# Nine gate tiles of the second mixer: from mixed matmuls of 512 and 256 columns to 256 columns alone

## The chip, the cores and the metric

The kernel runs on one core of one Trainium2 chip. The metric is the device time of one execution in microseconds. Before the change the median of three runs is 976.09 us (975.73 to 976.19).

## The reference, cut to what matters

The reference runs three transformer layers over 256 tokens of width 1024, all in float32: a layer with a short convolution and a gated MLP, a layer with windowed attention and a gated MLP, and a last layer with a hybrid mixer and an MLP. The change lies in the hybrid mixer:

```python
proj = jnp.einsum("bsd,dc->bsc", u, w_in)
q, k, v, x_lru, g_lru, gate_attn, gate_lru = jnp.split(proj, list(SPLITS), axis=-1)
...
attn = moba_attention(qh, kh, to_heads(v))
y_attn = attn @ w_branch_attn
xc = causal_depthwise_conv(x_lru, conv_w, conv_b)
hl = rg_lru(xc, w_rg_a, b_rg_a, w_rg_i, b_rg_i, lru_lambda)
y_lru = (hl * jax.nn.gelu(g_lru)) @ w_branch_lru
merged = jax.nn.sigmoid(gate_attn) * y_attn + jax.nn.sigmoid(gate_lru) * y_lru
return merged @ w_out
```

The three gates, `g_lru`, `gate_attn` and `gate_lru`, are each 1024 columns of the product with `w_in`. There are 8 heads of attention; with 256 tokens and blocks of 256 each head is plain causal attention.

## The kernel before, in words

**Products.** Activations lie with features on the 128 partitions and tokens along the columns. For float32 accuracy every operand is split into a high part, rounded to the matmul's input format, and a low part, the rest. A product is the sum of three: high weights with high activations, high weights with low activations, low weights with high activations. A tile is 128 output features for 256 tokens, summed over 8 blocks of 128 input features. High and low activations of a block lie next to each other, 256 columns each.

**Two kinds of tile.** A narrow tile has three matmuls of 256 columns for each of the 8 blocks, 24 in all, into one half of a PSUM bank (`blocks`, lines 549, 551 and 553). A mixed tile (`whole_tile`) does the two products with high weights at once for the first six blocks, as one matmul of 512 columns into the whole bank (line 524); the low weights (line 522) and the last two blocks (lines 533 and 534) go in 256 columns into the first half. So it has 6 matmuls of 512 columns and 12 of 256. The two halves of its bank still have to be added: ScalarE copies the second half into `spill` (`spill_tile`, line 1136), and VectorE adds the first half to it (`sum_tile`, line 1675). A narrow tile's result VectorE copies out of the bank by itself (line 2092).

**Weights.** Each tile has one piece of weights of 128 x 1024. ScalarE rounds it into `whi` (line 1104) and VectorE subtracts to get `wlo` (line 1638). There are four places for pieces; that of tile n + 4 is made when tile n is done. The first operation behind a tile on ScalarE is the spill, if the tile is mixed, and then the rounding of that piece.

**The order in the second mixer.** A loop over `r` (on TensorE from line 944 on; tiles 0 to 59) goes through the tiles of its input projection in a fixed order: `x2`, `q2`, `k2`, `rg`, `v2`, and then the gates `g2` (36 to 43), `ga` (44 to 51) and `gl` (52 to 59). `beside(r)` puts the steps of attention behind certain tiles: scores (lines 904 and 905) of a new head behind every third one from 33 to 54, values (lines 931 to 933) and transposes (line 916) of earlier heads there too, with the first transposes behind tile 37 and the last values behind tile 59. Such a set of small matmuls is called a group here. The loop is followed by two projections of 8 tiles each, `ba` (the first `MIXED_BRANCH` = 2 tiles are mixed) and `bl`, and by the output projection `out2`.

`MIXED_GATES` names the gate tiles that are mixed. Before the change it holds ten: 36, 37, 38, 40, 43, 46, 49, 52, 55 and 58. All of them but 36 stand right behind a group; groups stand behind tiles 36, 37, 39, 42, 45, 48, 51, 54, 57 and 59. The engines ask `is_mixed(r)`, and offsets into the count of spills (`S0`) follow from the list's length.

**Other places that the prediction names.** In the attention layer's mixer (called the first mixer here), blocks of its output projection (`wo_blocks`, narrow) stand behind transposes (line 798); the second half of that projection is narrow tiles alone. In the first part of the last MLP (`mup_first`, lines 1031, 1032 and 1038) narrow matmuls follow a group that spreads a row of gains (line 1012); mixed tiles follow them.

Of the kernel before, what the change touches and what calls it, by code (L numbers as in the profile page):

```python
# [53 lines left out]
for _name, _n in BODIES:  # L54
# [10 lines left out]
AT = {name: 4 * B0[name] - R0 for name in ("x2", "q2", "k2", "rg", "v2", "g2", "ga", "gl", "ba")}  # L65
HEAD_AT = AT["v2"] + 5

MIXED_GATES = [r for r in range(AT["g2"], AT["ba"])
               if r == AT["g2"] or (r - HEAD_AT) % 3 == 1 or r == HEAD_AT + 5]
MIXED_BRANCH = 2  # L70

S0 = {}
# [1 line left out]
for _name, _n in (("bx", 4 * WIDE_BODIES), ("up0", 4 * WIDE_BODIES), ("qkv", 12), ("up1", 4 * WIDE_BODIES),  # L74
                  ("x2", 8), ("q2", 8), ("k2", 8), ("gates", len(MIXED_GATES)), ("ba", MIXED_BRANCH),
                  ("out2", 7), ("mup", 4 * WIDE_BODIES)):
# [46 lines left out]
def build(nc, bias_in_dram, x_in, stream, vecs_in, sinks_in, cons_in, out):  # L123
    with ExitStack() as ctx:
# [263 lines left out]
        def segment_of(r):  # L388
            return [name for name in AT if AT[name] <= r][-1]
# [23 lines left out]
        def is_mixed(r):  # L413

            return segment_of(r) in S0 or r in MIXED_GATES

# [1213 lines left out]
        def _(dve):  # L1630
# [41 lines left out]
            def sum_tile(at, slot, dst):  # L1672

                dve.wait_ge(spilled, at + 1)
                dve.tensor_tensor(dst, acc(slot), spill[:, slot, :], ALU.add).then_inc(emptied, 1)  # L1675
# [376 lines left out]
            for r in range(AT["ba"]):  # L2052
# [18 lines left out]
                else:  # L2071
# [16 lines left out]
                    elif is_mixed(r):  # L2088
                        sum_tile(S0["gates"] + MIXED_GATES.index(r), r % 4, dst)
                    else:  # L2090
# [429 lines left out]
```

## Time and profile before

| | |
|---|---|
| median of 3 runs | 976.09 us (975.73 to 976.19) |
| the profiled execution | 975.92 us |
| its span on the core | 973.9 us |
| TensorE busy | 967.8 us (99%) |
| VectorE busy | 692.0 us (71%) |
| ScalarE busy | 583.1 us (60%) |
| GpSimd busy | 267.0 us (27%) |

The profile names the engines PE (TensorE's matmuls), PEld (its weight loads), DVE (VectorE), ACT (ScalarE) and POOL (GpSimd). L524 is line 524. Matmuls overlap: one of 256 columns is given as some 276 ns long, while the next begins some 113 ns after it. So the pace is read from the distance between starts, and the sum of the durations is more than the time that passed.

### The profile page before, as it was taken

Reading aid. Unit: us, or ns where it says so; the run is one execution under the profiler, and the core shown is the slowest. Engines: PE = TensorE matmul, PEld = TensorE weight load, DVE = VectorE, ACT = ScalarE, POOL = GpSimd, SP = SyncE. Lnnn points to the kernel's source line nnn. Section 1 sums busy time; section 2 is a strip of 40 time slices with the busy share of each in tenths; the row PEclk is TensorE's granted clock in tenths of the full one; section 3 lists DMA queues with packets and bytes.
Section 4 is the critical chain, followed back from the end, with each engine's and each line's share of the span. In section 5 each row is a group of like instructions: output and inputs, shape, how many; then the busy total and the mean of one; then the engine's idle time right before and its main releaser. Section 6 shows DMA issues by size and latency. Waiting matters only on the chain.

```text
span 973.9 us, 20479 instructions
## 1 busy us (share of the span) xinstructions
PE 967.8 (99%) x7368; PEld 913.1 (94%) x7368; DVE 692.0 (71%) x1037; ACT 583.1 (60%) x1026; POOL 267.0 (27%) x241
## 2 busy tenths in 40 slices
PE   9999999999999999999999999999999999999998
PEld 7999999999998899999999999889999999998887
DVE  6987866665668788666655799997866877664443
ACT  7556754454557767555554587968484677664332
POOL 2431233220102222322201146642031545441000
PEclk9999999999999999999999999999999999999999
DMA  9785555545543235555556555554445536556531
GB/s 332 261 316 188 189 208 180 207 171 196 205 169 136 88 130 217 179 209 184 182 193 210 179 177 172 200 196 168 168 144 181 202 130 221 209 176 206 182 130 44
DMA packets 37714, 180.96 MB, mean 186 GB/s; under 512 B 3472, under 2 KB 7824, under 8 KB 19984
## 3 DMA queue, kind: packets, MB, share of 16 engines
q1 hardware_dynamic: 37504, 179.99, 52.6%
q8 instruction: 43, 0.70, 0.3%
q14 instruction: 23, 0.19, 0.1%
q10 hardware_dynamic: 144, 0.08, 0.0%
HBM read 179.01 MB, written 1.05 MB: 185 GB/s over the span
## 4 chain that ended last, share of the span: by engine, by line
PE 91%; DVE 5%; ACT 2%; issue 1%; POOL 0%; ACTq 0%; POOLq 0%
PE bank L553 21%; PE bank L549 19%; PE bank L551 19%; PE bank L547 5%; PE bank L524 4%; PE bank L590 4%; PE bank L591 4%; PE bank L589 4%; PE bank L522 3%; DVE wlo L1638 3%; PE bank L673 1%; DVE z L1675 1%; PE bank L534 1%; PE bank L533 1%; DVE bank L2020 1%
## 5 line engine op out<-in xcount | busy, mean ns | idle before, releaser
L1638 DVE TENSOR_TENSOR wlo<-raw,whi 128x1024 fp32r<-128x1024 f32 (+1 forms) x289 | 354.5, 1227 | 153.9 <-ACT whi L1104 153.3
L1104 ACT ACTIVATE whi<-raw 128x1024 fp32r<-128x1024 f32 (+2 forms) x289 | 302.2, 1046 | 217.3 <-PE bank L553 210.6
L549 PE MATMUL bank<-xa,whi 128*128 128x256 f32 x952 | 239.4, 276 | 0.0
L551 PE MATMUL bank<-xa,whi 128*128 128x256 f32 x952 | 239.3, 276 | 0.0
L553 PE MATMUL bank<-xa,wlo 128*128 128x256 f32 x1184 | 236.4, 277 | 0.0
L553 PEld LDWEIGHTS bank<-xa,wlo 128*128 128x128 f32 x1184 | 187.0, 188 | 7.6
L549 PEld LDWEIGHTS bank<-xa,whi 128*128 128x128 f32 x952 | 178.7, 188 | 0.0
L551 PEld LDWEIGHTS bank<-xa,whi 128*128 128x128 f32 x952 | 178.7, 188 | 0.0
L2250 POOL TENSOR_TENSOR gate<-act,rbc 128x256 f32<-128x256 f32 x44 | 68.9, 1567 | 158.2 <-ACT act L1270 153.0
L551 PE MATMUL bank<-ghid,whi 128*128 128x256 f32 x352 | 88.5, 276 | 0.0
L549 PE MATMUL bank<-ghid,whi 128*128 128x256 f32 x352 | 88.5, 276 | 0.0
L549 PE MATMUL bank<-xb,whi 128*128 128x256 f32 x336 | 87.2, 281 | 0.2 <-ACT rr L1482 0.2
L551 PE MATMUL bank<-xb,whi 128*128 128x256 f32 x336 | 85.9, 277 | 0.0
L1647 DVE TENSOR_TENSOR wlo<-raw,whi 128x1024 fp32r<-128x1024 f32 x40 | 49.2, 1231 | 45.9 <-ACT whi L1114 45.8
L547 PE MATMUL bank<-xa,whi 128*128 128x512 f32 x232 | 77.1, 403 | 0.0
L1114 ACT ACTIVATE whi<-raw 128x1024 fp32r<-128x1024 f32 x40 | 42.5, 1066 | 49.3 <-PE bank L591 33.1
L553 PE MATMUL bank<-xb,wlo 128*128 128x256 f32 x336 | 69.1, 277 | 0.0
L553 PE MATMUL bank<-ghid,wlo 128*128 128x256 f32 x352 | 68.6, 276 | 0.0
L524 PE MATMUL bank<-xa,whi 128*128 128x512 f32 x240 | 68.4, 393 | 0.1
L549 PEld LDWEIGHTS bank<-ghid,whi 128*128 128x128 f32 x352 | 66.1, 188 | 0.0
L551 PEld LDWEIGHTS bank<-ghid,whi 128*128 128x128 f32 x352 | 66.1, 188 | 0.0
L2231 POOL TENSOR_TENSOR ssum<-ssum,sq 128x256 f32<-128x256 f32 x39 | 35.8, 917 | 106.9 <-ACT sq L1146 106.5
(258 smaller groups left out, 1817.8 us busy)
## 6 DMA issues: line engine op xcount, KB each, us to landing
raw<-in_stream SPq DMA_DIRECT2D x137, 1024.0 KB, 4.8
raw<-in_stream SPq DMA_DIRECT2D x42, 512.0 KB, 4.9
raw<-in_stream SPq DMA_DIRECT2D x8, 768.0 KB, 4.1
bias<-in_bias SPq DMA_DIRECT2D x1, 3072.0 KB, 11.5
raw<-in_stream SPq DMA_DIRECT2D x8, 256.0 KB, 5.0
x<-in_x SPq DMA_DIRECT2D x4, 256.0 KB, 4.9
out<-x SPq DMA_DIRECT2D x3, 256.0 KB, 2.2
cons<-in_cons SPq DMA_DIRECT2D x1, 576.0 KB, 9.5
```

What stands on the lines that cost most here:

```text
L524: pe.matmul(dst, whi[:, slot, k, :], X[:, k, :, :], start=k == 0, stop=False)
L547: pe.matmul(dst, whi[:, slot, at + i, :], X[:, k, :, :], start=first and i == 0, stop=False)
L549: pe.matmul(narrow, whi[:, slot, at + i, :], X[:, k, 0, :], start=first and i == 0, stop=False)
L551: pe.matmul(narrow, whi[:, slot, at + i, :], X[:, k, 1, :], start=False, stop=False)
L553: ins = pe.matmul(narrow, wlo[:, slot, at + i, :], X[:, k, 0, :], start=False, stop=last and i == len(tiles) - 1)
L589: pe.matmul(dst[:, :], X[:, k0 + k, 0, cols], hi, start=first and k == 0, stop=False)
L590: pe.matmul(dst[:, :], X[:, k0 + k, 0, cols], lo, start=False, stop=False)
L1104: act.activation(whi[:, p, 0:kts, :].rearrange("p k m -> p (k m)"), src, ACT.Copy)\
L1114: act.activation(dst[:, p, :, :].rearrange("p (k m) c -> p k m c", k=2), k_pairs(raw[:, (b % 2) * 2 + p // 2, :], p % 2), ACT.Copy).then_i ...
L1638: dve.tensor_tensor(wlo[:, p, 0:kts, :].rearrange("p k m -> p (k m)"), src, whi[:, p, 0:kts, :].rearrange("p k m -> p (k m)").bitcast(F32) ...
L1647: dve.tensor_tensor(lo[:, p, :, :].rearrange("p (k m) c -> p k m c", k=2), k_pairs(raw[:, (b % 2) * 2 + p // 2, :], p % 2), hi[:, p, :, :] ...
L2250: pool.tensor_tensor(gate[:, m, :], act1[:, m, :], rbc[:], ALU.mult).then_inc(gate_ready, 1)
```

## The change

The list of mixed gate tiles is cut to its first, tile 36. The nine others are computed as narrow tiles, on TensorE, ScalarE (no spill) and VectorE (a copy in place of the sum). Nothing else changes.

```diff
-MIXED_GATES = [r for r in range(AT["g2"], AT["ba"])
-               if r == AT["g2"] or (r - HEAD_AT) % 3 == 1 or r == HEAD_AT + 5]
+MIXED_GATES = [AT["g2"]]
 MIXED_BRANCH = 2
```

## Rows read from the trace of the kernel before

**Rows 1.** The page's head: span, and busy time of each engine.

```profile
span 973.9 us, 20479 instructions
PE 967.8 (99%) x7368; PEld 913.1 (94%) x7368; DVE 692.0 (71%) x1037; ACT 583.1 (60%) x1026; POOL 267.0 (27%) x241
```

**Rows 2.** The page's chain of waits: shares of the span by engine.

```profile
PE 91%; DVE 5%; ACT 2%; issue 1%; POOL 0%; ACTq 0%; POOLq 0%
```

**Rows 3.** Busy time by windows, tiles 37 to 59, all engines.

```profile
core 0: us, PE busy (x) PEld busy (x) DVE busy (x) ACT busy (x) POOL busy (x), PEclk, DMA share, GB/s
643.98:719.12 75.14, 75.14 (x596) 72.34 (x595) 59.67 (x112) 50.34 (x94) 14.37 (x16) 1.00 0.47 158
```

**Rows 4.** Timeline of TensorE, tiles 40 to 42: start, length, line, operation, count.

```profile
654.12 0.49 PE L916 MATMUL bank<-cons,pr 128*128 128x128 f32 x3
654.37 0.95 PE L524 MATMUL bank<-xb,whi 128*128 128x512 f32 x3
655.16 0.63 PE L522 MATMUL bank<-xb,wlo 128*128 128x256 f32 x4
655.63 0.86 PE L524 MATMUL bank<-xb,whi 128*128 128x512 f32 x3
...
657.24 0.28 PE L549 MATMUL bank<-xb,whi 128*128 128x256 f32 x1
...
659.96 0.28 PE L549 MATMUL bank<-xb,whi 128*128 128x256 f32 x1
```

**Rows 5.** Timeline of TensorE, second tile of `ba`, mixed.

```profile
721.98 0.85 PE L524 MATMUL bank<-xa,whi 128*128 128x512 f32 x3
722.67 0.39 PE L522 MATMUL bank<-xa,wlo 128*128 128x256 f32 x2
```

**Rows 6.** Timeline of TensorE, tile 37, and the transposes behind it.

```profile
643.98 1.05 PE L524 MATMUL bank<-xb,whi 128*128 128x512 f32 x3
...
646.98 0.49 PE L916 MATMUL bank<-cons,pr 128*128 128x128 f32 x3
```

**Rows 7.** Timeline of TensorE, narrow matmuls behind transposes in the first mixer.

```profile
325.84 0.85 PE L798 MATMUL bank<-cons,pr 128*128 128x128 f32 x6
326.45 0.36 PE L549 MATMUL bank<-xb,whi 128*128 128x256 f32 x1
326.65 0.28 PE L551 MATMUL bank<-xb,whi 128*128 128x256 f32 x1
```

**Rows 8.** Timeline of TensorE, first part of the last MLP.

```profile
788.19 0.94 PE L1012 MATMUL bank<-cons,vecs 128*128 128x128 f32 x7
788.89 0.37 PE L1031 MATMUL bank<-xa,whi 128*128 128x256 f32 x1
789.10 0.28 PE L1032 MATMUL bank<-xa,wlo 128*128 128x256 f32 x1
...
798.64 0.40 PE L1038 MATMUL bank<-xa,whi 128*128 128x256 f32 x2
...
801.42 0.93 PE L524 MATMUL bank<-xa,whi 128*128 128x512 f32 x3
```

**Rows 9.** Groups of narrow matmuls: 789.1 to 798.7, 350.2 to 358.7, 643.98 to 719.12.

```profile
L1032 PE MATMUL bank<-xa,wlo 128*128 128x256 f32 x28 | 7.0, 279 | 0.0
...
L551 PE MATMUL bank<-xb,whi 128*128 128x256 f32 x24 | 6.2, 280 | 0.0
...
L551 PE MATMUL bank<-xb,whi 128*128 128x256 f32 x112 | 28.2, 276 | 0.0
```

**Rows 10.** Windows of TensorE alone: busy (count), clock, DMA share, GB/s.

```profile
345.80:358.70 12.90, 12.90 (x109) 1.00 0.44 157
789.10:798.70 9.60, 9.60 (x84) 1.00 0.31 112
```

**Rows 11.** Groups of ScalarE and VectorE, 643.98 to 719.12.

```profile
L1104 ACT ACTIVATE whi<-raw 128x1024 fp32r<-128x1024 f32 x23 | 24.3, 1056 | 9.1 <-PE bank L553 9.1
L1136 ACT ACTIVATE spill<-bank 128x256 f32<-128x256 f32 x10 | 3.8, 385 | 14.6 <-PE bank L522 14.6
L1638 DVE TENSOR_TENSOR wlo<-raw,whi 128x1024 fp32r<-128x1024 f32 x23 | 29.4, 1280 | 10.9 <-ACT whi L1104 10.9
L2092 DVE COPY gl<-bank 128x256 f32<-128x256 f32 x5 | 2.0, 409 | 0.0
L1675 DVE TENSOR_TENSOR gl<-bank,spill 128x256 f32<-128x256 f32 x3 | 1.3, 419 | 0.9 <-ACT spill L1136 0.9
```

**Rows 12.** Groups of TensorE, 609.4 to 611.7 (second quarter of `rg`).

```profile
L551 PE MATMUL bank<-xb,whi 128*128 128x256 f32 x8 | 2.0, 276 | 0.0
```

**Rows 13.** Groups of TensorE, 804.3 to 815 (last MLP).

```profile
L551 PE MATMUL bank<-xa,whi 128*128 128x256 f32 x8 | 2.0, 276 | 0.0
```

## The prediction

> **What bounds the kernel now.** I read the page first: TensorE is busy for 99% of the span, VectorE for 71%, ScalarE for 60% [rows 1]. A busy TensorE proves little, since the ends of matmuls are modelled, so next comes the chain of what ended last: 91% of it is TensorE [rows 2]. Then the stretch that the change touches, from tile 37 to the end of tile 59 of the second mixer (643.98 to 719.12 us): TensorE is busy for all of its 75.14 us, at a granted clock of 1.00 (the 2.4 GHz level), with 59.7 us of VectorE and 50.3 us of ScalarE beside it [rows 3]. Last the starts of single matmuls, because a stretch that TensorE fills can only become shorter or longer by their pace. The narrow tile from 657.24 to 659.96 takes 2.72 us for 24 matmuls of 256 columns, 113.3 ns each, with no gap [rows 4]. So the stretch is bound by the issue of matmuls, and nothing in front of them is late.
>
> **What the change does to TensorE's work.** It turns nine of the ten mixed tiles (37, 38, 40, 43, 46, 49, 52, 55, 58) into narrow ones. A mixed tile is 6 matmuls of 512 columns and 12 of 256, a narrow one 24 of 256. Both stream 6,144 columns. In the steady state a 512-column matmul costs what two of 256 cost: three of them, from 721.98 to 722.67, take 0.69 us, 230 ns each, against 2 x 113.3 = 227 [rows 5]. By the columns alone the change moves nothing, and by this row a narrow tile is even cheaper by 6 x 3 = 18 ns; 9 x 18 ns = 0.16 us is the most that this term could save.
>
> **What stands behind the groups.** Each of the nine follows a group of small matmuls of attention (128 to 256 columns). The mixed tile behind such a group, from 654.37 to 657.24, takes 2.87 us [rows 4] (the eight tiles of this kind lie between 2.86 and 2.87; I use 2.865), 0.145 us more than a narrow one in steady state. Tile 37, behind a group of scores only, takes 643.98 to 646.98, 3.00 us [rows 6].
>
> What a narrow tile costs there is not in this stretch, as no narrow tile follows a group, but three others show its parts.
> - The start. Narrow matmuls behind a group of transposes occur in the first mixer: from the first to the second there are 0.20 us (326.45 to 326.65) [rows 7], 0.088 more than 0.113. A mixed tile has about 0.09 there as well, since its start costs the same switch. Behind scores only I take what tile 37 has over a tile at the slower pace below, 3.00 - 2.72 - 24 x 0.0045 = 0.17 us, bounded below by 0.09.
> - The pace after the start. In the first part of the MLP, narrow matmuls follow a group of 128-column ones. From 789.10 to the first of the two that start at 798.64 there are 81 steps in 9.54 us: 117.8 ns each, not 113.3 [rows 8]. They stay at that pace until their run ends; nothing brings them back. The duration that the profile gives shows the same two paces: 279 ns in that stretch, 280 ns in the second half of the first mixer's output projection (350.2 to 358.7, three narrow tiles one behind the other), 276 ns in the stretch that the change touches [rows 9]. The clock is granted in full in all three [rows 3, 10]. So TensorE has two paces for a stream of narrow matmuls, 4% apart, and a stream that begins slow stays slow.
> - The way back. Behind a group the mixed tile begins at the slow pace too (its first four narrow matmuls, 655.16 to 655.63, take 117.5 ns each [rows 4]), but by its end it is at the fast one: the narrow tiles that follow it run at 276 ns [rows 9] and 2.72 us [rows 4]. I read this as the wide matmuls bringing the stream back. That is the part that goes.
>
> **The sum**, on the assumption that all narrow tiles from 37 to 59 now run at the slow pace (each group starts it anew):
> - 8 tiles behind groups with transposes: 0.201 + 23 x 0.1178 = 2.910 us against 2.865, +0.045 each, +0.36.
> - 14 tiles that were narrow already (39; two in each of six spans between groups; 59): 24 x 0.1178 = 2.827 against 2.72, +0.107 each, +1.50.
> - Tile 37: 0.113 + 0.17 + 23 x 0.1178 = 2.99 against 3.00, -0.01; with the lower bound of its start, -0.09.
>
> Together +1.85 us on TensorE (+1.77 with the lower bound of tile 37's start). The bounds of the pace are 113.3 (the steady row: the stream is fast at once) and 117.8; with 113.3 the three terms are 8 x (0.201 + 23 x 0.1133 - 2.865) = -0.46, 0, and 0.17 + 2.72 - 3.00 = -0.11, together -0.57 us. I take 117.8 because the nearest rows, narrow matmuls behind 128-column groups, all have it: five runs of 7 matmuls or more behind transposes in the first mixer, of which one is in rows 7, and the long one of rows 8.
>
> The Trainium skill, "TensorE: Matmul & The Clock Gate", section "Wait — 56ns, not 53.3ns?", gives one warm step for a matmul: its columns at 2.4 GHz plus about 2.5 ns. By that rule 9 x 6 further matmuls would cost an estimated 0.14 us and no stream could be slow at a full clock. This trace disagrees: 113.3 and 117.8 ns stand side by side for 256 columns [rows 4, 8].
>
> **The other engines.** ScalarE loses nine copies of half a bank into the spill buffer, 9 x 0.385 = 3.5 us; VectorE's nine sums of bank and spill (0.42 us) become nine copies (0.41 us) that need not wait for the spill [rows 11]. I cost this at nothing: TensorE is what hides it. The weights of tile n + 4 are rounded when tile n is done (1.06 us on ScalarE, then 1.28 us on VectorE) [rows 11] and are wanted three tiles, over 8 us, later. These engines only get more room. If TensorE were waiting for them, each tile would give back up to 0.385 us; no row shows such a wait. No DMA is added or moved, and no wait: the copy waits for the same matmul that the spill waited for. ScalarE's next piece of weights waits for it too.
>
> **Sum against the runs.** The profiled execution took 975.92 us (span 973.9), so 977.77 after. The median of the three runs is 976.09, 0.17 above it: 977.9. A difference of 0.2% (1.95 us, about what a measurement of this kernel can tell from no change) lies just above the forecast difference.
>
> **Rivals.**
> 1. *The narrow stream is fast, or gets fast by itself.* A narrow tile that started behind a semaphore wait and not behind a group ran at 276 ns at once (609.4 to 611.7) [rows 12], so the slow pace isn't a must. The page's single step would lead here. Then -0.57 us: 975.5. This is the case that ends on the other side; it decides at the second matmul of each tile behind a group. Against it: rows 7 and 8. A milder form is that the slow pace ends after some eight matmuls, a third of a tile, as in the mixed tiles: 8 x (2.72 + 0.088 + 0.03 - 2.865) = -0.2 and -0.1 for tile 37, so 975.8.
> 2. *The slow pace outlives the stretch.* Tile 0 of the next projection stays mixed and follows a group. If it doesn't bring the pace back, the 6 narrow tiles left of that projection and the 8 narrow ones of the next stay slow: 14 x 0.107 = 1.5 us more, 979.4. Against it: behind the slow narrow matmuls four mixed tiles begin at 801.42 [rows 8], and the narrow ones that follow them run at 276 ns [rows 13].
> 3. *The change frees the engines beside TensorE and this shows.* It would need waits of TensorE in this stretch. There are none [rows 3, 4]; a gain of 9 x 0.385 = 3.5 us (972.6) would have to come from there.
>
> **How the numbers follow.** Slow pace throughout: 0.79. Rival 1: 0.13 for both forms. Rival 2: 0.06. Rival 3: 0.02. The likeliest case alone spans 977.4 to 978.4: half a nanosecond of pace is 0.3 us over its 23 x 24 matmuls, the starts are open by 0.1 us, and the three runs differ by up to 0.5 us. The range takes in a mix of slow and fast groups, which lies between 975.5 and 977.9, down to 976.6, and part of the way to rival 2, up to 978.9; about 0.15 is left out. Slower by over 0.2% is beyond 978.04: 0.43 of the likeliest case (0.34) and rival 2, 0.40. Faster by over 0.2% is rival 3: 0.02. Within: 0.58.
>
> **What would show it.** After the change the rows of narrow matmuls between 644 and 721 us should give 279 ns instead of 276, and each of the 14 narrow tiles that were there before 2.83 us instead of 2.72. The tiles behind groups should take 2.91 us and the stretch about 77.0 us instead of 75.14. Behind it, the narrow tiles should be back at 276 ns after the mixed tile. The forecast is wrong if these rows stay at 276 ns, or if TensorE's starts show gaps.

## The result: slower by 0.16%, and the profile after

| | before | after |
|---|---|---|
| median of 20 runs each | 976.04 us | 977.59 us |
| lowest to highest | 975.61 to 976.51 | 977.20 to 978.11 |
| ratio, 95% interval | | 1.0016 (1.0010 to 1.0022) |
| profiled execution (span) | 975.92 us (973.9) | 977.58 us (975.7) |

The difference is 1.55 us; 1.85 was forecast, with 977.9 us and a range of 976.6 to 978.9.

The page's head of the changed kernel answers [rows 1]. All the matmuls are one line earlier in this kernel (L548 for L549, L523 for L524).

```profile
span 975.7 us, 20578 instructions
PE 969.6 (99%) x7422; PEld 917.2 (94%) x7422; DVE 693.2 (71%) x1037; ACT 581.3 (60%) x1017; POOL 265.9 (27%) x241
```

There are 54 more matmuls (9 tiles x 6) and nine instructions fewer on ScalarE, the spills. The stretch from tile 37 to the end of tile 59, by windows, answers [rows 3]:

```profile
core 0: us, PE busy (x) PEld busy (x) DVE busy (x) ACT busy (x) POOL busy (x), PEclk, DMA share, GB/s
644.12:720.95 76.83, 76.83 (x650) 76.50 (x649) 60.42 (x112) 48.06 (x85) 14.62 (x16) 1.00 0.45 157
```

It took 75.14 us and takes 76.83, at the same granted clock. These 1.69 us are the difference: the medians differ by 1.55, the two profiled spans by 1.8. ScalarE works 2.3 us less in it, and TensorE is no faster for that.

TensorE's timeline of tiles 40 to 42 of the changed kernel answers [rows 4]: start, length, line, operation, count.

```profile
654.24 0.49 PE L915 MATMUL bank<-cons,pr 128*128 128x128 f32 x3
654.48 0.37 PE L548 MATMUL bank<-xb,whi 128*128 128x256 f32 x1
654.69 0.28 PE L550 MATMUL bank<-xb,whi 128*128 128x256 f32 x1
...
657.40 0.28 PE L548 MATMUL bank<-xb,whi 128*128 128x256 f32 x1
...
660.22 0.28 PE L548 MATMUL bank<-xb,whi 128*128 128x256 f32 x1
...
663.05 0.38 PE L903 MATMUL bank<-k,q 128*128 128x128 f32 x2
```

Tile 40, behind the group, takes 2.92 us; tiles 41 and 42, whose instructions the change does not touch, take 2.82 and 2.83 instead of 2.72. The groups of narrow matmuls of the changed kernel answer [rows 9]. The first row is of tile 37 (644.5 to 647.1), the second of tiles 38 and 39 (647.7 to 652.9), the third of tiles 40 to 59 (655.0 to 720.3), and the last of the narrow tiles behind the stretch (724.5 to 730).

```profile
L550 PE MATMUL bank<-xb,whi 128*128 128x256 f32 x8 | 2.1, 279 | 0.0
...
L550 PE MATMUL bank<-xb,whi 128*128 128x256 f32 x16 | 4.0, 276 | 0.0
...
L550 PE MATMUL bank<-xb,whi 128*128 128x256 f32 x159 | 40.9, 279 | 0.0
...
L550 PE MATMUL bank<-xa,whi 128*128 128x256 f32 x10 | 2.5, 276 | 0.0
```

The slow pace is there as forecast, in 21 of 23 tiles, and it ends behind the mixed tiles of the next projection. Tiles 38 and 39 are the exception: they run fast.

### The profile page after: what moved, and what is told of

The parts are those of the page before. It is cut to its first block, busy times and chain, and to the rows that moved or that the text cites. A ratio compares the mean times of both kernels' runs of the same rounds, so it can differ in the third digit from the quotient of the medians.

```text
span 975.7 us, 20578 instructions
## 1 busy us (share of the span) xinstructions
PE 969.6 (99%) x7422; PEld 917.2 (94%) x7422; DVE 693.2 (71%) x1037; ACT 581.3 (60%) x1017; POOL 265.9 (27%) x241
## 4 chain that ended last, share of the span: by engine, by line
PE 96%; DVE 2%; ACT 1%; issue 1%; POOL 0%; POOLq 0%
PE bank L552 22%; PE bank L548 20%; PE bank L550 19%; PE bank L523 6%; PE bank L546 5%; PE bank L521 4%; PE bank L588 4%; PE bank L589 4%; PE bank L590 4%; PE bank L533 1%; PE bank L532 1%; PE bank L672 1%; PE bank L797 1%; DVE wlo L1637 1%; DVE xa L1692 1%
## 5 line engine op out<-in xcount | busy, mean ns | idle before, releaser
L548 PE MATMUL bank<-xa,whi 128*128 128x256 f32 x952 | 239.4, 276 | 0.0
L548 PEld LDWEIGHTS bank<-xa,whi 128*128 128x128 f32 x952 | 178.7, 188 | 0.0
L548 PE MATMUL bank<-xb,whi 128*128 128x256 f32 x408 | 107.2, 283 | 0.1
L550 PE MATMUL bank<-xb,whi 128*128 128x256 f32 x408 | 105.0, 278 | 0.0
L548 PE MATMUL bank<-ghid,whi 128*128 128x256 f32 x352 | 88.5, 276 | 0.0
L552 PE MATMUL bank<-xb,wlo 128*128 128x256 f32 x408 | 83.8, 278 | 0.0
L548 PEld LDWEIGHTS bank<-xb,whi 128*128 128x128 f32 x408 | 76.5, 188 | 1.8 <-issue 1.3
L550 PEld LDWEIGHTS bank<-xb,whi 128*128 128x128 f32 x408 | 76.7, 188 | 0.0
L523 PE MATMUL bank<-xa,whi 128*128 128x512 f32 x240 | 68.4, 393 | 0.1
L548 PEld LDWEIGHTS bank<-ghid,whi 128*128 128x128 f32 x352 | 66.1, 188 | 0.0
```

What stands on the lines that cost most here:

```text
L523: pe.matmul(dst, whi[:, slot, k, :], X[:, k, :, :], start=k == 0, stop=False)
L548: pe.matmul(narrow, whi[:, slot, at + i, :], X[:, k, 0, :], start=first and i == 0, stop=False)
L550: pe.matmul(narrow, whi[:, slot, at + i, :], X[:, k, 1, :], start=False, stop=False)
L552: ins = pe.matmul(narrow, wlo[:, slot, at + i, :], X[:, k, 0, :], start=False, stop=last and i == len(tiles) - 1)
```

## The experiments

The theory: behind a group the narrow stream starts at 117.8 ns a step, stays there, and wide matmuls (512 columns) bring it back to 113.3. The rivals: the pace belongs to the attention stretch and to what the other engines do in it; it is a matter of chance at each start; wide matmuls have no part in it; ScalarE and VectorE have a share in the difference. All ratios below are against the kernel before, run on the same chip.

**The change on TensorE alone** (`narrow_spilled`): the nine tiles' matmuls in 256 columns, with the spill and the sum kept.

```diff
-                            whole_tile(r % 4, xb, acc(r, True), 4).then_inc(piece_done, 1)
+                            if r == AT["g2"]:
+                                whole_tile(r % 4, xb, acc(r, True), 4).then_inc(piece_done, 1)
+                            else:
+                                two_halves(r % 4, xb, acc(r, True)).then_inc(piece_done, 1)
...
+            def two_halves(slot, X, dst):
+                narrow, apart = dst[:, 0:TOK], dst[:, TOK:2 * TOK]
+                for k0 in range(0, KT, 2):
+                    for k in (k0, k0 + 1):
+                        pe.matmul(narrow, whi[:, slot, k, :], X[:, k, 0, :], start=k == 0, stop=False)
+                        pe.matmul(apart, whi[:, slot, k, :], X[:, k, 1, :], start=False, stop=False)
+                    for k in (k0, k0 + 1):
+                        ins = pe.matmul(narrow, wlo[:, slot, k, :], X[:, k, 0, :], start=False, stop=k == KT - 1)
+                return ins
```

> The kernel before, with the nine tiles' matmuls all in 256 columns as in the changed kernel, but high weights with low activations into the second half of the bank, so that ScalarE still spills and VectorE still sums: the change on TensorE alone. Theory (all of the difference is TensorE's pace): as the changed kernel, 977.6 within 0.4. Rival (freeing ScalarE and VectorE gave something back in the changed kernel, up to 9 x 0.385 us): up to 3.5 us above it.

Measured: 977.64 us, ratio 1.0016 (1.0007 to 1.0025). From the first matmul of tile 37 to the end of tile 59 there are 76.83 us, the same as in the changed kernel. So the difference is TensorE's alone; the nine spills and sums are worth nothing here, as no wait of TensorE hung on them (the trace has none in the stretch).

**A group far from attention** (`probe0`): three 128-column matmuls on constants in front of the first MLP's down projection.

```diff
                     if c == 0:
                         pe.wait_ge(emptied, tile - 3)
+                    if q == 0 and name == "dn0":
+                        for _ in range(3):
+                            pe.matmul(bank[ATT][:, 0:P], con("ones", P), cons[:, 0:P], start=True, stop=True)
```

> The kernel before, with a group of three matmuls of 128 columns on constants (result unused) in front of the first narrow tile of the first MLP's down projection, far from attention; 528 narrow matmuls follow with no mixed tile between. Theory: this alone starts the slow pace and it lasts to the end of the projection: 279 ns, 528 x 4.5 ns = 2.4 us and about 0.4 for the group itself, +2.8 us, 978.9. Rival (the slow pace belongs to the attention stretch, to what the other engines do there): 276 ns, +0.4 us, 976.4. A third: the start is a matter of chance, as tile 38 of the changed kernel started fast; then either of the two.

Measured: 979.1 us, ratio 1.0031 (1.0019 to 1.0044). The groups of TensorE over that projection, first in the kernel before (216.9 to 275.0):

```profile
L551 PE MATMUL bank<-ghid,whi 128*128 128x256 f32 x171 | 43.0, 276 | 0.0
```

and in this one (216.9 to 279.5):

```profile
L551 PE MATMUL bank<-ghid,whi 128*128 128x256 f32 x176 | 45.2, 279 | 0.0
```

Three small matmuls slow the 528 that follow, over 62 us, with no attention near. The theory holds in its first half, and the rival of the place falls. The difference to the kernel before is 3.2 us, 0.4 over the forecast, mostly because the group costs more than I took: on float32 constants the three matmuls are six records of the profile (0.59 us from the first to the narrow tile's start), and 0.09 us go for the start, 0.68 in place of 0.4.

**Is the start always slow, and does the size of the group decide?** (`groups_of_3`, `groups_1_to_12`): the same in front of every second piece of that projection, with 3 matmuls each, or 1, 2, ... 12.

```diff
+                    if q % 2 == 0 and name == "dn0":
+                        i = q // 2
+                        for _ in range(3):   # the other kernel: range(i + 1)
+                            pe.matmul(bank[ATT][:, 0:P], con("ones", P), cons[:, 0:P], start=True, stop=True)
```

> The kernel before, with a group of three 128-column matmuls on constants (result unused) in front of every second piece of the first MLP's down projection: 12 groups, each followed by 36 or 48 narrow matmuls. Theory as forecast (a group always starts the stream slow): 12 of 12 streams at 117.8 ns a step; 12 x 0.42 us for the groups and 528 x 4.5 ns = 2.4 us, +7.4 us, 983.3. Rival (the pace is drawn anew at each start, as tile 38 of the changed kernel shows): some of the 12 streams at 113.3 ns, each some 0.2 us less.

> The same 12 places, with groups of 1, 2, 3, ... 12 matmuls. Theory: all streams slow, whatever the size; 78 x 0.11 + 12 x 0.09 + 2.4 = +12.1 us, 988.0. Rival (the size of the group decides the pace, for instance odd or even): fast and slow streams sorted by size.

Measured, one execution each: 986.48 and 995.86 us. In the starts of single matmuls all 24 streams step at 117.8 ns from the second matmul to their end. The groups over all twelve places, `groups_of_3` first, `groups_1_to_12` behind it:

```profile
L551 PE MATMUL bank<-ghid,whi 128*128 128x256 f32 x164 | 42.1, 279 | 0.0
...
L551 PE MATMUL bank<-ghid,whi 128*128 128x256 f32 x148 | 38.1, 280 | 0.0
```

Behind these groups the start is slow every time, whatever their size. But a group is not needed for it. In the kernel before, the four narrow tiles of `rg` have no group near, begin with a first step of 0.19 to 0.22 us, and run slow, fast, fast and slow. The second is that of [rows 12]; this is the first (606.5 to 609.0):

```profile
L551 PE MATMUL bank<-xb,whi 128*128 128x256 f32 x8 | 2.1, 279 | 0.0
```

Both times of these two runs are above the forecast by the doubled records of the groups: for 12 x 3 matmuls 12 x 0.68 us and 2.4 us for the pace make 10.6, and 10.4 was measured.

**Do wide matmuls bring the stream back?** (`probe2`): two of 512 columns behind the group of `probe0`.

```diff
+                        for _ in range(2):
+                            pe.matmul(bank[ATT][:, 0:2 * TOK], whi[:, 0, 0, :], ghid[:, 0, :, :], start=True, stop=True)
```

> As the kernel with the group of three in front of the down projection, with two matmuls of 512 columns (result unused) between the group and the first narrow tile. Theory (wide matmuls bring the stream back): 276 ns in the projection; the group 0.4 us, two wide matmuls 0.46 us, +0.9 us, 977.0. Rival (wide matmuls don't bring it back; a mixed tile does it by something else, or six are needed): 279 ns, +3.3 us, 979.3.

Measured: 979.53 us, ratio 1.0036 (1.0022 to 1.0049), narrow matmuls at 279 ns. Two do not.

**The second tile behind the group mixed, not the first** (`mixed_second`), an edit of the changed kernel:

```diff
-MIXED_GATES = [AT["g2"]]
+MIXED_GATES = [r for r in range(AT["g2"], AT["ba"])
+               if r == AT["g2"] or (r > AT["g2"] + 4 and (r - HEAD_AT) % 3 == 2)]
```

> The changed kernel, but the SECOND tile behind each full group is mixed (41, 44, 47, 50, 53, 56, 59), the first stays narrow. Theory (a narrow stream that starts slow stays slow until wide matmuls bring it back): the first tiles 40, 43, ... at 279 ns and 2.91 us, the third ones 42, 45, ... 57 back at 276 ns and 2.72 us; per three tiles 2.91 + about 2.78 + 2.72 = 8.41 us against 8.56 in the changed kernel, 6 x 0.15, about 0.9 us less than the changed kernel: some 976.7, 0.6 above the kernel before. Rival (the pace is set once, at the first matmul behind the group, and lasts to the next group; wide matmuls don't alter it): third tiles at 279 ns, time as in the changed kernel, 977.6.

Measured: 977.13 us, ratio 1.0012 (1.0003 to 1.0021), between the two forecasts. Tile 42, behind the mixed tile 41 (660.2 to 662.8), and tile 54, behind the mixed tile 53 (700.4 to 703.0):

```profile
L551 PE MATMUL bank<-xb,whi 128*128 128x256 f32 x8 | 2.0, 276 | 0.0
...
L551 PE MATMUL bank<-xb,whi 128*128 128x256 f32 x8 | 2.1, 279 | 0.0
```

Four mixed tiles (41, 44, 47, 50) brought the stream back and three (53, 56, 59) did not. So wide matmuls can do it, and something else decides whether they do. The trace shows a difference in front of them: the groups before the three are longer than those before the four, by 0.11, 0.01 and 0.09 us. The transposes that end the group in front of tile 40, and in front of tile 52:

```profile
654.22 0.49 PE L916 MATMUL bank<-cons,pr 128*128 128x128 f32 x3
...
694.20 0.55 PE L916 MATMUL bank<-cons,pr 128*128 128x128 f32 x3
```

By the starts of single matmuls the narrow streams behind all seven groups step at 117.8 ns, but their first step is 207 ns for the four and 201 or 202 for the three, and the mixed tile's first three wide matmuls step at 234, 235 and 230 ns for the four and some 230, 231 and 226 for the three. So there is more than one way to run slow; that this is what decides fits all seven tiles, but no run sets it apart.

**How many wide matmuls?** (`groups_then_wide`): at the twelve places groups of three, followed by 0, 1, ... 11 wide matmuls.

```diff
+                        for _ in range(i):
+                            pe.matmul(bank[ATT][:, 0:2 * TOK], whi[:, n % 4, 0, :], ghid[:, 0, :, :], start=True, stop=True)
```

> The same 12 places, groups of three, each followed by 0, 1, 2, ... 11 matmuls of 512 columns (result unused) before the narrow ones. Theory in its first form (wide matmuls bring the stream back): from some number on, at most six, all streams at 113.3 ns. Rival, after the second tiles of mixed_second (four brought the stream back, three did not) and the two wide matmuls that did not: no number does it for certain, fast and slow streams lie mixed over 0 to 11. Time: 12 x 0.42 + 66 x 0.23 = 20.2 us, and up to 2.4 for the pace: 996 to 998.5.

Measured: 1001.14 us. The mean step of the narrow stream behind, from the starts of 28 matmuls each:

```
wide matmuls   0      1      2      3      4      5      6      7      8      9      10     11
ns a step      117.7  117.8  117.8  117.7  113.4  117.8  117.8  113.4  117.7  117.8  113.3  117.8
```

Fast and slow streams lie mixed, as the rival had it, but in an order that neither expectation had: 4, 7 and 10 bring the stream back, no other number does, each tried once here. The time is 2.6 us above the expected range for the same reason as in the two runs before, the doubled records of the groups. The timeline shows the two neighbours, 4 and 5, with the narrow matmuls behind them:

```profile
241.95 1.18 PE L661 MATMUL bank<-ghid,whi 128*128 128x512 f32 x4
242.97 0.28 PE L549 MATMUL bank<-ghid,whi 128*128 128x256 f32 x1
...
249.00 1.41 PE L661 MATMUL bank<-ghid,whi 128*128 128x512 f32 x5
250.24 0.28 PE L549 MATMUL bank<-ghid,whi 128*128 128x256 f32 x1
```

and the groups of the narrow matmuls behind 4 (242.9 to 248.5) and behind 5 (250.2 to 254.3):

```profile
L551 PE MATMUL bank<-ghid,whi 128*128 128x256 f32 x16 | 4.0, 276 | 0.0
...
L551 PE MATMUL bank<-ghid,whi 128*128 128x256 f32 x12 | 3.1, 279 | 0.0
```

In a run of wide matmuls the steps, from start to start, go round in threes (226, 230 and 231 ns after the first ones), so that every third one ends in the same place of that round: the runs of 4, 7 and 10 end on a step of 231 to 233 ns, those of 5, 8 and 11 on 225, those of 6 and 9 on 229 and 230. The run of 3, still among the first steps, ends on 231 too and stays slow.

**The count put to the test in the gate tiles** (`wide4`, `wide5`, `wide7`): the nine tiles begin with that many wide matmuls; their other blocks are narrow. One kernel is shown, the others differ in the last argument.

```diff
+            def wide_first(slot, X, dst, wide):
+                narrow = dst[:, 0:TOK]
+                for k in range(wide):
+                    pe.matmul(dst, whi[:, slot, k, :], X[:, k, :, :], start=k == 0, stop=False)
+                for k in range(wide):
+                    pe.matmul(narrow, wlo[:, slot, k, :], X[:, k, 0, :], start=False, stop=False)
+                for k in range(wide, KT):
+                    pe.matmul(narrow, whi[:, slot, k, :], X[:, k, 0, :], start=False, stop=False)
+                    pe.matmul(narrow, whi[:, slot, k, :], X[:, k, 1, :], start=False, stop=False)
+                    ins = pe.matmul(narrow, wlo[:, slot, k, :], X[:, k, 0, :], start=False, stop=k == KT - 1)
+                return ins
...
-                            whole_tile(r % 4, xb, acc(r, True), 4).then_inc(piece_done, 1)
+                            if r == AT["g2"]:
+                                whole_tile(r % 4, xb, acc(r, True), 4).then_inc(piece_done, 1)
+                            else:
+                                wide_first(r % 4, xb, acc(r, True), 4).then_inc(piece_done, 1)
```

> The kernel before, but each of the nine tiles begins with exactly 4 matmuls of 512 columns (its first four blocks), and all else in it is in 256. Theory after the twelve places with 0 to 11 wide matmuls (behind a group the narrow stream comes back where 4, 7 or 10 wide ones follow the start, and not elsewhere): tiles 40 to 59 at 276 ns from the fifth matmul of the first tile on; tile behind a group about 2.83 us against 2.865, 8 x 0.03 us less than before: 975.8. Rival (the wide matmuls of the probe and of real tiles differ, or the share of wide matmuls counts: 4 are fewer than the 6 of before): 279 ns, 977.6.

> The same with 5 wide matmuls in front. Theory (4, 7, 10): 5 do not bring the stream back, tiles 40 to 59 at 279 ns, about the time of the changed kernel, 977.6, although more matmuls are wide than with 4. Rival (more wide matmuls help more): 276 ns, 975.8.

> The same with 7 wide matmuls in front. Theory (4, 7, 10): back at 276 ns after the seventh, 975.8. Rival (what 4 did was chance, or wide matmuls in one run do nothing): 279 ns, 977.6.

| | median | ratio to before, 95% interval | tile 37 to the end of 59 |
|---|---|---|---|
| `wide4` | 975.84 us | 0.9997 (0.9988 to 1.0006) | 74.87 us |
| `wide5` | 977.69 us | 1.0017 (1.0008 to 1.0026) | 76.80 us |
| `wide7` | 976.11 us | 0.9999 (0.9990 to 1.0008) | 74.91 us |

The narrow matmuls of tiles 40 to 59 (655.8 to 718.0) with 4, 5 and 7 wide ones in front:

```profile
L564 PE MATMUL bank<-xb,whi 128*128 128x256 f32 x104 | 26.2, 276 | 0.0
...
L564 PE MATMUL bank<-xb,whi 128*128 128x256 f32 x98 | 25.3, 280 | 0.0
...
L564 PE MATMUL bank<-xb,whi 128*128 128x256 f32 x101 | 25.4, 276 | 0.0
```

All three came out as the count says, at every group from tile 40 on. Five wide matmuls cost 1.85 us more than four, with the same spills and sums and fewer instructions on TensorE. Tile 37, behind scores alone, goes the other way round: its narrow matmuls are at 276 ns with 5 and at 279 with 4 and 7. So the number that works is not the same behind every group; this rests on one tile in each kernel.

`wide4` is faster than the changed kernel by 1.75 us. Against the kernel before its 0.2 us are within the interval; the stretch of the profile, 74.87 us against 75.14, has the 8 x 0.03 us that were expected.

**The same elsewhere** (`wide4_wo`): 4 wide matmuls also at the start of the second half of the attention layer's output projection, whose 96 narrow matmuls, with the 12 in front of them, ran at the slow pace before.

```diff
                         pe.wait_ge(half_lo, 2)
-                        blocks(p, xb, range(0, 4), acc(p), True, False)
+                        for k in range(4):
+                            pe.matmul(acc(p, True), whi[:, p, k, :], xb[:, k, :, :], start=k == 0, stop=False)
+                        for k in range(4):
+                            pe.matmul(acc(p), wlo[:, p, k, :], xb[:, k, 0, :], start=False, stop=False)
```

with a spill of that tile on ScalarE and its sum on VectorE.

> As the kernel with 4 wide matmuls, and the same at the start of the second half of the attention layer's output projection, where 108 narrow matmuls ran at 117.8 ns before; that tile gets a spill and a sum. Theory (4 wide matmuls behind any start bring the stream back): up to 104 x 4.5 ns = 0.45 us less than with 4 alone, 975.4, rows there at 276 ns. Rival (the count holds for a start behind a group only; here the stream starts behind a wait): 280 ns as before, 975.8.

Measured: 976.19 us, ratio 1.0002 (0.9993 to 1.0011). The narrow matmuls there (345.8 to 358.7) stay slow, as the rival had it, and the time is above both expectations.

```profile
L565 PE MATMUL bank<-xb,whi 128*128 128x256 f32 x32 | 8.3, 279 | 0.0
```

The rival's reason, a start behind a wait, is not what the run has. The timeline shows the last narrow matmul of the first half and the four wide ones:

```profile
346.90 0.28 PE L567 MATMUL bank<-xb,wlo 128*128 128x256 f32 x1
347.01 1.08 PE L901 MATMUL bank<-xb,whi 128*128 128x512 f32 x4
```

There is no gap between them: 12 narrow matmuls at the slow pace run right up to the four wide ones. So what failed here is 4 in the middle of a slow stream, where three mixed tiles of `mixed_second` failed too. The count behind a start with no group remains untried.

**Another end of the group** (`order_values_last`): the changed kernel with the transposes in front of the values.

```diff
-                if valued_head(r) is not None:
-                    values2(valued_head(r))
                 if turned_head(r) is not None:
                     turn2(turned_head(r))
+                if valued_head(r) is not None:
+                    values2(valued_head(r))
```

> The changed kernel, with the transposes of a group in front of its values, so that matmuls of the values stand last. Theory (any group of small matmuls starts the stream slow): tiles 40 to 59 at 279 ns, time as in the changed kernel, 977.6 within 0.3. Rival (it is the transposes as the last of the group that start it slow): 276 ns from tile 40 on, 14 x 0.107 and 8 x 0.1 less, about 975.6.

Measured: 979.01 us, ratio 1.0032 (1.0020 to 1.0044), slower than both expectations. Moved forward, the transposes now wait for VectorE's probabilities, as the waits of TensorE from 652 to 716 us say (who waits, for whom, us in total, times, longest):

```profile
PE bank L915 <- DVE pr L1993: 0.7, 3, 0.3
```

By the starts of single matmuls five groups are drawn out by 1.9 us in all, more than these waits show; less some 0.5 us for the streams that ran fast, that makes the 1.4 us over the changed kernel. What the run was for it half answers: behind two of the drawn-out groups the stream was fast (tiles 40 to 42 and 58 to 59), behind three slow, and behind the two groups with no wait slow. The narrow matmuls of tiles 40 to 42 (654.8 to 662.7):

```profile
L550 PE MATMUL bank<-xb,whi 128*128 128x256 f32 x24 | 6.0, 276 | 0.0
```

So a group does not always start the stream slow; which of the drawn-out ones do, no run explains.

## Why the prediction was right, step by step

- *TensorE's pace alone decides.* Shown: [rows 3] against the window after, and `narrow_spilled`, which keeps the other engines' work and costs the same.
- *By the columns the change moves nothing.* Shown by `wide4` and `wide7`: with 4 or 7 of 8 blocks wide the stretch has the same length to 0.04 us.
- *A narrow tile behind a group starts slow and stays slow.* Right for tile 37 and tiles 40 to 59 (2.92, 2.82 and 2.83 us; 2.91 and 2.827 forecast), and outside the stretch in 24 of 24 places. The rows before did not force it, though: [rows 12] is the fast one of two fast and two slow tiles of `rg`, and the five runs behind transposes in the first mixer are four of nine matmuls each by the trace. That all seven starts from tile 40 on came out slow was in part luck, as two of these seven were fast in `order_values_last`. Not right for tiles 38 and 39, behind a group of three transposes alone that follows a slow tile: 276 ns, in this kernel and in three others that begin the stretch alike. Forecast were +0.045 for tile 38 and +0.107 for tile 39; in the changed kernel they have 0.201 + 23 x 0.1133 - 2.865 = -0.06 and 0. That is 0.21 us of the sum, and 1.64 is what is left of 1.85, against 1.69 in the stretch. Why that one group starts fast is open.
- *Tile 37.* 3.01 us (644.13 to 647.14), 2.99 forecast.
- *Wide matmuls bring the stream back, and that is the part that goes.* Right for the kernel before, where all eight mixed tiles behind transposes do it; too simple as a rule. Behind a full group, or a group on constants, it is the number of wide matmuls after the start that decides: of those tried, 4, 7 and 10 in a row, and not 5, although it is more than 4. The six of a mixed tile come as three, four narrow ones and three, and that pattern works behind a full group and failed in three of seven tiles where it began in the middle of a slow stream (`mixed_second`).
- *Behind the stretch the pace comes back.* Right: 276 ns from 724.5 on, so rival 2 did not happen.
- *Rival 3, room for the other engines.* Did not happen: ScalarE has 2.3 us less to do in the stretch, and TensorE nothing to wait for.
- The Trainium skill's one warm step per matmul ("TensorE: Matmul & The Clock Gate", section "Wait — 56ns, not 53.3ns?") would have given an estimated 0.14 us. At a granted clock of 1.00 the same instruction steps at 113.3 or at 117.8 ns here, so the measurement decides against it.

The chance for slower by over 0.2% was 0.40 and that for within 0.2% was 0.58; the measured 0.16% lies within, and its interval is clear of no change. The prediction took 0.2% for about what a measurement can tell from no change; the interval here reaches 0.06% to either side.

## What to carry to other kernels

Where TensorE is the bound, read the distance between the starts of equal matmuls before anything else: a few per cent of pace over a long stream cost more than the instructions that an edit adds or removes. After an edit compare that step also in the tiles that the edit does not touch: most of this change's price was paid by tiles that it left alone. A tile whose form looks arbitrary may be there for the state in which it leaves the engine, and only trying the neighbouring numbers (4, 5, 7) shows which part of it does the work.

## What the runs showed that I had not expected

- In 24 of 24 places a group of small float32 matmuls put the stream of 256-column matmuls into the slow one of its two paces (117.8 and not 113.3 ns, at a granted clock of 1.00), and it stayed there for as long as the narrow stream lasted: 528 matmuls and 62 us in `probe0`.
- Behind such a group 4, 7 or 10 matmuls of 512 columns brought it back; 0, 1, 2, 3, 5, 6, 8, 9 and 11 did not. Behind scores alone 5 did, and 4 and 7 did not, in one tile each. In the middle of a slow stream 4 did not. What in the engine goes round in threes no run shows.
- A matmul of 128 columns on float32 constants is two records of the profile, some 0.11 us each; a transpose of the same size is one.
